# mLSTM outputs: the inter-chunk part weighed on GpSimd, local and inter products summed in one PSUM place, VectorE normalising from it

## The reference, cut to what matters

```
w_inter = exp(a_inter - m_t)
s   = exp(d - m_t) * (q_c . k_c)                 # local, within the chunk
num = w_inter * (C . q_c) + s . v_c             # inter-chunk + local
den = w_inter * (n . q_c) + sum(s)
h   = num / max(|den|, exp(-m_t))
C_new = decay * C + (wg * v_c) . k_c ;  n_new likewise
```

## Time and profile before

| what | us |
|---|---|
| median of 3 runs (3364.49 to 3364.69) | 3364.52 |
| the profiled execution | 3362.84 |
| its span in the profile | 3361.1 |
| core, mean granted TensorE clock | core 0, 0.975 |
| TensorE matmul busy | 3229.5 (96%) |
| VectorE busy | 2024.4 (60%) |
| ScalarE busy | 1324.9 (39%) |
| GpSimd busy | 446.2 (13%) |

### The profile page before, as it was taken

One profiled execution on the slowest core, in us unless ns is written; L12 is line 12 of the kernel. 1 busy time (PEld: TensorE's weight loads), 2 busy tenths in 40 slices (PEclk: granted clock), 3 DMA queues, 4 the chain that ended last, 5 costly groups with the idle time before them and its releaser, 6 DMA issues. The chain is left out here.

```text
span 3361.1 us, 39601 instructions
## 1 busy us (share of the span) xinstructions
PE 3229.5 (96%) x16006; PEld 2691.1 (80%) x16006; DVE 2024.4 (60%) x2591; ACT 1324.9 (39%) x2011; POOL 446.2 (13%) x495
## 2 busy tenths in 40 slices
PE   6999999999999889999999999979999999999998
PEld 3788888878788779878888888867879987787987
DVE  7555555545664788665565555555238886425885
ACT  4222222233334458532222222372128854213872
POOL 0001100112011112120101101001102300110330
PEclk8999999999999689999999999989999999999999
DMA  5222222226255268312222222224426512444451
GB/s 203 88 88 76 88 88 76 88 76 115 97 185 171 84 119 117 85 51 75 101 88 84 88 80 84 74 52 135 129 77 84 96 40 71 147 123 84 59 90 63
DMA packets 140725, 320.69 MB, mean 95 GB/s; under 512 B 55824, under 2 KB 72976, under 8 KB 129536
## 3 DMA queue, kind: packets, MB, share of 16 engines
q1 hardware_dynamic: 86000, 232.48, 24.0%
q0 software_dynamic: 54544, 85.68, 10.7%
HBM read 261.52 MB, written 51.10 MB: 93 GB/s over the span
## 5 line engine op out<-in xcount | busy, mean ns | idle before, releaser
L2137 DVE TENSOR_TENSOR w_lo<-w_raw,w_hi 128x1024 fp32r<-128x1024 f32 (+1 forms) x126 | 211.4, 1678 | 310.7 <-ACT w_hi L1539 310.7
L873 PE MATMUL psum<-a_hi,w_hi 128*128 128x512 f32 x704 | 276.3, 392 | 5.7 <-DVE a_lo L2259 3.8
L873 PE MATMUL psum<-a_lo,w_hi 128*128 128x512 f32 x704 | 274.9, 391 | 0.0
L873 PE MATMUL psum<-a_hi,w_lo 128*128 128x512 f32 x704 | 274.8, 390 | 0.0
L2612 DVE TENSOR_TENSOR attn_tl<-psum,attn_th 128x512 fp32r<-128x512 f32 x384 | 246.1, 682 | 5.1 <-ACT attn_th L1885 3.8
L2327 DVE SCALAR_TENSOR_TENSOR x<-psum,cols,x 128x1024 f32<-128x1024 f32 x144 | 184.4, 1282 | 94.5 <-PE psum L873 94.3
L1885 ACT ACTIVATE attn_th<-psum 128x512 fp32r<-128x512 f32 x384 | 209.2, 598 | 68.2 <-PE psum L1281 64.5
L1539 ACT ACTIVATE w_hi<-w_raw 128x1024 fp32r<-128x1024 f32 (+1 forms) x126 | 174.2, 1382 | 131.4 <-PE psum L873 39.6
L1281 PEld LDWEIGHTS psum<-mats,attn_num 128*128 128x128 f32 x1536 | 179.1, 141 | 34.5 <-issue 8.2
L1281 PE MATMUL psum<-mats,attn_num 128*128 128x128 f32 x1536 | 201.4, 274 | 5.4 <-DVE attn_tl L2612 4.9
L3273 POOL TENSOR_TENSOR sq<-w_raw 128x256 f32<-128x256 f32 x40 | 30.3, 759 | 1174.6 <-DMA w_raw<-in_w_gu 1162.9
(11 more groups left out here) (573 smaller groups left out, 8453.6 us busy)
## 6 DMA issues: line engine op xcount, KB each, us to landing
w_raw<-in_w_ada SPq DMA_DIRECT2D x52, 1024.0 KB, 5.0
w_raw<-in_w_gu SPq DMA_DIRECT2D x44, 1024.0 KB, 4.9
w_raw<-in_w_in SPq DMA_DIRECT2D x34, 1024.0 KB, 5.1
w_raw<-in_w_down SPq DMA_DIRECT2D x22, 1024.0 KB, 4.9
w_raw<-in_w_out SPq DMA_DIRECT2D x12, 1024.0 KB, 7.5
qk_hi_scratch<-p_out_hi POOLq DMA_DIRECT2D x18, 512.0 KB, 3.0
qk_lo_scratch<-p_out_lo POOLq DMA_DIRECT2D x18, 512.0 KB, 3.8
w_early<-in_w_ada SPq DMA_DIRECT2D x8, 1024.0 KB, 18.1
```

What stands on the lines that cost most here:

```text
L873: mm = e.matmul(bank, a[:, k * width + m * P:k * width + (m + 1) * P], b(k, h), start=(ends[0] and k == order[0] and i == 0), stop=(ends[1 ...
L2137: e.tensor_tensor(like(src, lo), src, like(src, hi.bitcast(F32)), ALU.subtract).then_inc(*w_done.mark(n, part))
```

## The change

The weight of the inter-chunk part is put on the queries ahead of the product, by GpSimd, and no longer on the product by VectorE. The rows of `w_inter` (rows 64 to 99 of `QA`) are stored to DRAM by SP and loaded back, one row broadcast over the 64 partitions of a head, into two new tiles `qw`; GpSimd multiplies them by the queries in place (`weigh_queries`), for head 0 ahead of `causal(1)`, for the others behind the `causal` of the same head. TensorE then puts the local and the inter-chunk product of a chunk into the same PSUM columns, alternating; a group takes one place instead of two, and starts only when both the local and the inter operands are there. The place is emptied by the final normalising instruction, event `h`, where it was emptied by `num`. `num` and its two instructions go. ScalarE reads |den| from PSUM as soon as TensorE is done. For direction 1, four `scalar_tensor_tensor` (one per chunk) divide and add in one pass. In `causal` a wait for the last weighing is added. Two memory tiles swap places, which changes no instruction.

```diff
 tensor program, ml_outputs
             for dr in range(2):
                 for c0 in (0, 4):
-                    pl = ps.take(e, ("ml l", h, dr, c0), ml_dve, "num", h, dr, c0)
+                    p = ps.take(e, ("ml l", h, dr, c0), ml_dve, "h", h, dr, c0)
                     e.wait_ge(*ml_dve.at("S", h, dr))
-                    for c in range(c0, c0 + 4):
-                        mm = e.matmul(pl.full[:, (c % 4) * 256:(c % 4) * 256 + M_V + 1], m.E[i][dr][:, c, :],
-                                      m.v1[c // 4][:, c % 4, h, :], start=True, stop=True)
-                    mm.then_inc(*ml_pe.mark("l", h, dr, c0))
-                    pi = ps.take(e, ("ml i", h, dr, c0), ml_dve, "inter", h, dr, c0)
                     e.wait_ge(*ml_dve.at("C", h, 4, dr))
+                    e.wait_ge(*ml_scaled.at(h, dr))
                     for c in range(c0, c0 + 4):
                         j = c if dr == 0 else ST - 1 - c
-                        mm = e.matmul(pi.full[:, (c % 4) * 256:(c % 4) * 256 + M_V + 1], qt[part, c * P:(c + 1) * P],
-                                      m.C[part, dr, j, :], start=True, stop=True)
-                    mm.then_inc(*ml_pe.mark("i", h, dr, c0))
+                        to = p.full[:, (c % 4) * 256:(c % 4) * 256 + M_V + 1]
+                        local = e.matmul(to, m.E[i][dr][:, c, :], m.v1[c // 4][:, c % 4, h, :], start=True, stop=False)
+                        inter = e.matmul(to, m.qw[dr][part, c * P:(c + 1) * P], m.C[part, dr, j, :], start=False, stop=True)
+                    local.then_inc(*ml_pe.mark("l", h, dr, c0))
+                    inter.then_inc(*ml_pe.mark("i", h, dr, c0))
 scalar program, ml_outputs
-                    e.wait_ge(*ml_dve.at("num", h, dr, c0))
-                    e.activation(de[:, 0:4].unsqueeze(2), nu[:, :, M_V:M_V + 1], ACT.Abs).then_inc(*ml_act.mark("abs", h, dr, c0))
+                    e.wait_ge(*ml_pe.at("i", h, dr, c0))
+                    if dr:
+                        e.wait_ge(*ml_dve.at("h", h, 0, c0))
+                    elif h:
+                        e.wait_ge(*ml_dve.at("h", h - 1, 1, c0))
+                    e.activation(m.dn[n % 2][:, 0:4].unsqueeze(2), sums, ACT.Abs).then_inc(*ml_act.mark("abs", h, dr, c0))
 vector program, ml_outputs
-                    e.wait_ge(*ml_pe.at("i", h, dr, c0))
-                    e.tensor_tensor(nu[:], pi3, m.colsA[:, c0:c0 + 4, 64 + row:64 + row + 1].to_broadcast([P, 4, M_V + 1]),
-                                    ALU.mult).then_inc(*ml_dve.mark("inter", h, dr, c0))
-                    e.wait_ge(*ml_dve.now())
-                    e.tensor_tensor(nu[:], nu[:], pl3, ALU.add).then_inc(*ml_dve.mark("num", h, dr, c0))
                     yield
...
-                        e.tensor_tensor(dst, nu[:, :, 0:M_V], rb, ALU.mult).then_inc(*ml_dve.mark("h", h))
+                        e.tensor_tensor(dst, p3[:, :, 0:M_V], de[:, 8:12].unsqueeze(2).to_broadcast([P, 4, M_V]),
+                                        ALU.mult).then_inc(*ml_dve.mark("h", h, dr, c0))
                     else:
-                        e.tensor_tensor(nu[:, :, 0:M_V], nu[:, :, 0:M_V], rb, ALU.mult).then_inc(*ml_dve.mark("back", h))
-                        e.wait_ge(*ml_dve.now())
-                        e.tensor_tensor(dst, dst, nu[:, :, 0:M_V], ALU.add).then_inc(*ml_dve.mark("h", h))
+                        for c in range(4):
+                            e.scalar_tensor_tensor(out=dst[:, c, :], in0=p3[:, c, 0:M_V], scalar=de[:, 8 + c:9 + c],
+                                                   in1=dst[:, c, :], op0=ALU.mult, op1=ALU.add).then_inc(
+                                *ml_dve.mark("h", h, dr, c0))
 gpsimd program, causal and mlstm
+                if h:
+                    e.wait_ge(*ml_scaled.now())
+        def weigh_queries(h):
+            m, part = t.ml, slice(64 * (h % 2), 64 * (h % 2) + 64)
+            e.wait_ge(*ml_qk[h // 2].at(h // 2))
+            e.wait_ge(*ml_masked.now())
+            for dr in range(2):
+                e.wait_ge(*ml_w_in[2 * (h % 2) + dr].at(h))
+                e.tensor_tensor(m.qw[dr][part, :], m.qw[dr][part, :], m.qk[h // 2][part, :], ALU.mult).then_inc(
+                    *ml_scaled.mark(h, dr))
+            weigh_queries(0)
             causal(1)
+            weigh_queries(1)
...
                     causal(h + 2)
+                    weigh_queries(h + 2)
 sync program, mlstm
+            def inter_rows(h):
+                part = slice(64 * (h % 2), 64 * (h % 2) + 64)
+                for dr in range(2):
+                    if h >= 2:
+                        e.wait_ge(*ml_pe.at("i", h - 2, dr, 4))
+                    e.dma_start(m.qw[dr][part, :], d.ml_w[32 * dr + h].unsqueeze(0).to_broadcast([64, S])).then_inc(
+                        *ml_w_in[2 * (h % 2) + dr].mark(h))
+            e.wait_ge(*ml_act.at("rows ready"))
+            e.dma_start(d.ml_w[:, :], t.proj1.QA[64:64 + ROWS, :]).then_inc(*w_stored.mark())
             p1b_stored("tile", 9, 0)
             e.dma_start(m.qk[2][:], d.proj[10]).then_inc(*ml_qk[2].mark(2))
+            e.wait_ge(*w_stored.at())
...
             e.dma_start(m.qk[0][:], d.proj[8]).then_inc(*ml_qk[0].mark(0))
+            inter_rows(0)
             for dr in range(2):
                 minus_M(m.nb[dr], 1, dr, 2 + dr)
+            inter_rows(1)
...
                     minus_M(m.nb[dr], h, dr, 2 + dr)
+                inter_rows(h)
```

More of the change, by code:

```diff
@@ L489, in memory @@
     with ExitStack() as sc:
-        m.qk = [sb(f"ml_{n}", [P, S], F32, sc) for n in ("q0", "q1")] + [None, sb("ml_k1", [P, S], F32, sc)]
+        m.qk = [sb(f"ml_{n}", [P, S], F32, sc) for n in ("q0", "q1")] + [None, None]
         m.C = sb("ml_C", [P, 2, ST, M_V + 1], F32, sc)
         m.nb = rings("ml_minus_M", 2, [P, ST, P], F32, sc)
-        gap("ml_0", 32 * 1024 - 28 * 1024 - 64, sc)
+        m.qw = [sb("ml_qw0", [P, S], F32, sc)]
+        m.qk[3] = sb("ml_k1", [P, S], F32, sc)
         m.ktok = sb("ml_ktok", [P, ST, 256], F32, sc)
@@ L497, in memory @@
         m.v1 = rings("ml_v", 2, [P, 4, M_HEADS, M_V + 1], F32, sc)
-        m.num = rings("ml_num", 2, [P, 4, M_V + 1], F32, sc)
-        gap("ml_1", 65 * 1024 + 512 - 60 * 1024 - 128 - 4 * 1024 - 32, sc)
+        m.qw.append(sb("ml_qw1", [P, S], F32, sc))
+        gap("ml_1", 65 * 1024 + 512 - 60 * 1024 - 4 * 1024 - 192, sc)
         m.E = [[sb(f"ml_E0{d}", [P, ST, P], F32, sc) for d in range(2)]]
@@ L635, in scratch @@
     d.ml_nm = nc.dram_tensor("ml_minus_M", [ROWS, S], F32).ap()
+    d.ml_w = nc.dram_tensor("ml_inter", [ROWS, S], F32).ap()
     d.inv = nc.dram_tensor("inverse_sums", [3, A_HEADS * ST, P], F32).ap()
@@ L672, in program_of @@
     x_turned, z_turned = signal("x_turned", "PE"), signal("z_turned", "PE")
-    ml_masked, w_sums = (signal(n, "Pool") for n in ("ml_masked", "w_sums"))
+    ml_masked, w_sums, ml_scaled = (signal(n, "Pool") for n in ("ml_masked", "w_sums", "ml_scaled"))
     cs_done, w_hi, squared, guessed = (signal(n, "ACT") for n in ("cs_done", "w_hi", "squared", "guessed"))
@@ L697, in program_of @@
     ml_qk, ml_v = loaded("ml_qk_in", "SP", 4), loaded("ml_v_in", "SP", 2)
+    w_stored, ml_w_in = signal("ml_inter_stored", "SP", 16), loaded("ml_inter_in", "SP", 4)
     ml_stored3 = signal("ml_last_stored", "SP", 16)
@@ L1830, in ml_outputs @@
                 for c0 in (0, 4):
-                    nu, de = m.num[n % 2], m.dn[n % 2]
-                    e.wait_ge(*ml_dve.at("num", h, dr, c0))
-                    e.activation(de[:, 0:4].unsqueeze(2), nu[:, :, M_V:M_V + 1], ACT.Abs).then_inc(*ml_act.mark("abs", h, dr, c0))
+                    sums = ps.of[("ml l", h, dr, c0)].full.rearrange("p (c v) -> p c v", c=4)[:, :, M_V:M_V + 1]
+                    e.wait_ge(*ml_pe.at("i", h, dr, c0))
[4 more added lines that the diff above has]
+                    e.activation(m.dn[n % 2][:, 0:4].unsqueeze(2), sums, ACT.Abs).then_inc(*ml_act.mark("abs", h, dr, c0))
                     n += 1
@@ L1841, in ml_norm @@
             for f in range(2):
-                e.wait_ge(*ml_dve.at("h", h))
+                e.wait_ge(*ml_dve.at("h", h, 1, 4))
                 if h:
@@ L2522, in ml_outputs @@
                 for c0 in (0, 4):
-                    pi3, pl3 = (ps.of[(w, h, dr, c0)].full.rearrange("p (c v) -> p c v", c=4)[:, :, 0:M_V + 1]
-                                for w in ("ml i", "ml l"))
-                    nu, de = m.num[n % 2], m.dn[n % 2]
-                    e.wait_ge(*ml_pe.at("i", h, dr, c0))
-                    e.tensor_tensor(nu[:], pi3, m.colsA[:, c0:c0 + 4, 64 + row:64 + row + 1].to_broadcast([P, 4, M_V + 1]),
-                                    ALU.mult).then_inc(*ml_dve.mark("inter", h, dr, c0))
-                    e.wait_ge(*ml_dve.now())
-                    e.tensor_tensor(nu[:], nu[:], pl3, ALU.add).then_inc(*ml_dve.mark("num", h, dr, c0))
+                    p3 = ps.of[("ml l", h, dr, c0)].full.rearrange("p (c v) -> p c v", c=4)
+                    de = m.dn[n % 2]
```

2 lines of the change are left out of this document (removed).

## The result

The changed kernel takes 3377.26 us (median of 7 runs, 3374.36 to 3389.45) against 3364.52 for the kernel before on the same chip: a ratio of 1.0039, 95% interval 1.003 to 1.0049. That is 13 us slower, inside the range on record (3354 to 3379) and at its upper end, on the side that had been given 0.31; one of the seven runs, 3389.45, lies beyond it. One run among all of this document, of the last experiment, took 3590.48 us at a mean granted clock of 0.857, where the others of its kernel had 0.978 to 0.981; it is left out of every figure.

What follows compares the result with a forecast made beforehand. Bound: TensorE and VectorE handing work back and forth, neither full, TensorE mostly at half clock in the heads. Heads 9.6 + 2.2 + 0.5 - 9.6 = +2.7 us on 3362.84, 3365.5, median about 3367; range 3354 to 3379.

Steps and rivals of the forecast that it cites:

- the side that had been given 0.31: Whole kernel: slower by over 0.2% (6.7 us), chance 0.31; faster had 0.22, within had 0.47.
- a late store: Projection's last store, delayed by the extra DMA traffic: 0 to 2.2 us, taken as 0, 2.2 kept for the range.
- What is removed: VectorE: two instructions per group go, 22.2 us, and direction 1 saves 3 us; some 25 of 91 us lost.
- rival 3: GpSimd's eight products each meet a waiting maximum at the shared port: +9 to +19 us, 3374 to 3383; chance 0.10.
- What is added on GpSimd and SP: Eight GpSimd products of 2.365 us, 18.9 in all; nine DMAs on SP's queue, delaying the last store 0 to 2.2.
- TensorE's alternation: Same matmuls, alternated: between nothing and 0.2 us per group, 3 in all, if each switch lost overlap; taken as 0.
- Head 0, plus 9.6 or 3.4: First group starts at 1102.6, key transposes end at 1132.4: plus 9.6 us at half clock, plus 3.4 at full.
- the early clock: Rival 1: clock returns early because TensorE's work is denser; -7.8 us in all, 3357; chance 0.18.
- Head 1, plus 2.2: Group 4 waits 3.7 us for group 3's place, emptied by `h`; earlier |den| returns 1.3: plus 2.2 us.
- Head 2, plus 0.5: States to head end 20.9 us, waits for `h` against VectorE's savings: plus 0.5; minus 1.6 full clock, plus 2.9 half.
- Head 3, minus 9.6: First group starts early with almost no gap, clock stays full, last `h` at +10.4: minus 9.6 us; half clock minus 2.6.
- Rival 2: Kept clock doesn't come; waits for `h` put heads 2 and 3 at half clock: +12 us, 3377; chance 0.22.

Runs made afterwards that it cites:

- the last experiment: The run of the banks in turn: the best version with a group's chunks in the order 0, 2, 1, 3; 3348.22 us.
- the grouped order: Changed kernel, but each group does four local products, then four inter-chunk ones, into the same PSUM columns: 3363.74 us, ratio 1.0003.
- the best version: Changed kernel with grouped products, weighings of heads 0 and 1 and mask of head 1 earlier on GpSimd, group 3 normalised early: 3347.24 us, ratio 0.9948.
- the version with early normalising alone: Changed kernel, but VectorE normalises group 3 of each head right after group 2, ahead of the last states and S: 3377.74 us, ratio 1.0022.
- the banks in turn: The best version with chunks in the order 0, 2, 1, 3, so neighbours write different PSUM banks: 3348.22 us, ratio 0.9946.
- the run with alternation in one form: Kernel before, alternating, with the second product of each pair replaced by one on 128 rows, inter-chunk part left out: 3364.04 us.
- the kernel with half the switches: Changed kernel with the order inter, local, local, inter, twice in a group, four switches instead of seven: 3369.72 us.

## Why the prediction was right or wrong

The range held the result and the chance of slower was given 0.31, but the forecast, +2.7 us, missed 10 us of the 13. That the range held is in part luck: head 0 was put 5.7 us too high and head 3 13.2 too low, and the range's upper end came from half clock and a late store, not from the longer groups. By its steps:

- *What is removed:* right. VectorE lost 28.7 us, forecast 25. Four small instructions in a row take 1.13 us, not 0.95, where the two before took 1.38, so the instructions give 22.2 + 8 x 0.25 = 24.2; the other 4.5 are shorter waits beside GpSimd (rival 3 below).
- *What is added on GpSimd and SP:* right. A weighing is 2.3 us. GpSimd waited 9.04 us for the last store, against 8.82: of 0 to 2.2 for the extra traffic, 0.2.
- *TensorE's alternation:* this is the term that failed. The prediction had "between nothing and, if each switch were to lose overlap, 0.2 us per group" and took 0; it is 1.2 at full clock and 1.8 at half, six and nine times the upper bound. The bound came from no row; 0.2 us is what one switch costs at full clock, and a group has six more. The kernel before had the price in it, indirectly: at half clock eight rows of products take 2.02 us when the blocks on both sides have another form (1147.28), and 1.86 when the block ahead of them, the key transposes, has their own (these two rows).

```profile
1122.64 1.93 PE L1227 MATMUL psum<-ml_v,ml_E 128*128 128x129 f32 x8
1124.50 1.39 PE L1234 MATMUL psum<-ml_C,ml_q 64*128 64x129 f32 x8
```

  The two runs that add or take away this alone move the time by +14.8 and -13.5.
- *Head 0, plus 9.6 or 3.4:* the keys end 4.9 us later, 3.9 without the 1.0 from ahead of the stage. The start came as worked out (1103.7, forecast 1102.6 with a stage that began 1.0 earlier). The clock came back at about 1112, with the kv rows, and not 15 us later: the case that I had called the early clock, +3.4, and longer groups within it. The likelier case was the wrong one.
- *Head 1, plus 2.2:* from the keys' end to the states of head 2 it is 45.1 us against 42.0, +3.1, with the idle time of 3.9 us that was forecast as 3.7.
- *Head 2, plus 0.5:* 20.1 against 20.4 us, -0.4.
- *Head 3, minus 9.6:* +3.6. This is where the forecast went wrong, by 13 us. Group 1 did start early, after an idle time of 0.56 us. But the clock fell at 1191, with no gap but that one since 1176.91, and stayed at half through the unbroken work up to 1214; four groups took 5.8 us each. In the grouped order, at half clock too, head 3 takes 16.5, so 7.1 are the switches (4 x 1.76) and the rest, against 10.1 in the best version, is the clock. At half clock and with short groups I had 17.4, at full clock 10.4: both were measured in other kernels, 16.5 and 10.1. So two things failed in this step, in near equal parts: the length of the groups (7.1 us), and the premise that a start with almost no gap keeps the clock (6.4). The early start itself was right.
- *Rival 2* gave the number, 3377, but not the reason: it took the half clock to follow from idle times over 3 us ahead of head 3; it came after 0.56. It also had head 0 at +9.6, which was +3.9, and half of what it puts down to the clock in head 3 is the switching; its number is luck. *Rival 3:* three maxima waited and took 0.97, 0.67 and 1.14 us in place of 0.16, 2.3 lost in sum, not 9 to 19. The kernel before lost more at the same port, 1.9 and 4.9 us in the two instructions of the earlier trace rows, since its last addition had two SBUF operands and met both masks.

What stays open: why the clock falls in one execution and not in another where the rows before are alike. The 12 runs of the version with early normalising alone fall into two heaps 16 us apart. Whether shorter groups and fewer waits narrow it is not shown: the best version spreads over 4.5 us, but in five runs, and over 8.9 in three with the banks in turn. None of the runs here shows what decides. So the switches are shown as the cause of the longer groups and, by adding and removing them, of some 13 us; how that comes out of the group's length and the clock together is not. The 2.6 us behind the stage are in the spread between runs.

## What to carry to other kernels

Accumulating two products in PSUM is only as cheap as the order in which TensorE sees them: keep matmuls of one form together (open each bank once, run all of one kind, then add all of the other), since each change between 128 and 64 rows costs nearly as much as a matmul of this size (0.20 us beside 0.22 at full clock). Read such a price from the steps between rows and not from a block's mean, which mixes steps within the form with the one out of it. When an engine on the path loses work and the time doesn't fall, compare the busy time of the engine whose work was supposed to be the same. A PSUM place that is given free by a later instruction of a list must be checked against everything that stands ahead of that instruction in the list.

## What the runs showed of the hardware that was not expected

VectorE's wait for the port that it shares with GpSimd goes on over instructions of GpSimd that follow each other without a wait between, also when it begins inside the first of them. GpSimd and VectorE of the grouped kernel, order of time:

```profile
1163.34 4.66 POOL L3093 TENSOR_TENSOR ml_minus_M<-ml_minus_M,ml_mats 128x1024 f32<-128x1024 f32 x2
```

```profile
1114.13 2.23 DVE L2533 TENSOR_TENSOR ml_den<-ml_den,ml_colsB 128x4 f32<-128x4 f32 x1 [0.27 <-ACT ml_den L1839]
...
1165.12 2.92 DVE L2533 TENSOR_TENSOR ml_den<-ml_den,ml_colsB 128x4 f32<-128x4 f32 x1 [3.21 <-ACT ml_den L1839]
```

The maximum at 1165.12 begins within the first of two masks (1163.34 to about 1165.7) and ends at 1168.04, just after the second, which ends at 1168.00. It then gets in ahead of the next pair, which a semaphore wait holds back by about 0.13 us. The Trainium skill, SBUF — State Buffer, "Who interferes with whom", has whoever issues first hold the port for its whole instruction; these rows say for a run of them. What the prediction took from that rule for the new normalising instructions, which read one operand from PSUM, holds: the changed kernel's `hs` at 1115.74 takes its usual 0.69 us beside a mask.

The 64 columns of "kv" seem to count as a form of their own, though it works on 128 rows like the local products: in the run with alternation in one form the first pair behind a kv block takes 0.33 us (1101.22 to 1101.55), the next ones 0.22. No run was made for this alone.

A change to the other half of the rows within the same form is another matter: where the queries' products of one head (rows 0 to 63) are followed by "s" of the other head (rows 64 to 127), their rows interleave in the trace. This is the end of a group and the start of "s" in the kernel with half the switches:

```profile
1116.77 0.58 PE L1237 MATMUL psum<-ml_C,ml_qw 64*128 64x129 f32 x1
1116.77 0.58 PE L1215 MATMUL psum<-ml_q,ml_k 64*128 64x128 f32 x1
1117.14 0.42 PE L1237 MATMUL psum<-ml_C,ml_qw 64*128 64x129 f32 x1
```
